# Gate and up weights of an expert loaded in four transfers of 1 MB instead of two of 2 MB

## What is computed

```python
    g_prob = jax.nn.softmax((t @ w_rg + b_rg).astype(jnp.float32), axis=-1)
    p_g, g_idx = lax.top_k(g_prob, 1)
    ...
    p_e, e_idx = lax.top_k(jax.nn.softmax(e_sel, axis=-1), TOP_K)
    ...
    for e in range(N_EXPERTS):
        hid = jax.nn.silu(t @ w_gate[e]) * (t @ w_up[e])
        y = y + ((hid * dense_w[:, e:e + 1]) @ w_down[e]).astype(jnp.float32)
```

## Time and profile before

| what | us |
|---|---|
| median of 3 runs | 1626.03 (1625.09 to 1627.09) |
| the profiled execution, its own time | 1628.22 |
| its span, first to last instruction | 1626.4 |
| first load issued by the loop over the ring | 1193.97 |
| last load of weights issued | 1583.16 |
| mean granted clock of TensorE, share of full | 0.962 |

### The profile page before, as it was taken

How to read it: one execution, slowest core, us unless ns; L and a number is a source line. 1 busy time by engine, 2 the same in 40 slices (tenths; PEclk the granted TensorE clock), 3 DMA queues, 4 the chain that set the end, 5 groups by cost and what they waited for, 6 DMA issues and landing times.

```text
span 1626.4 us, 28468 instructions
## 1 busy us (share of the span) xinstructions
PE 1491.8 (92%) x10825; PEld 1154.2 (71%) x10826; DVE 1005.2 (62%) x1858; ACT 702.5 (43%) x1216; POOL 67.3 (4%) x88
## 2 busy tenths in 40 slices
PE   8999999999999999999999999999989666676667
PEld 7888888888888888888888889887844333232333
DVE  6777788677777777788677777988643122212222
ACT  5555566555555555666455556846310000000000
POOL 0000040000001000030200000001000000000000
PEclk9999999999999999999999999999999788879888
DMA  9665374365555656373465545445999999999997
GB/s 318 208 205 181 113 239 136 106 224 187 193 181 179 209 181 196 94 245 116 154 218 194 180 173 169 160 139 188 389 391 427 429 429 428 429 428 429 428 429 310
DMA packets 153370, 407.86 MB, mean 251 GB/s; under 512 B 5712, under 2 KB 99264, under 8 KB 140000
## 3 DMA queue, kind: packets, MB, share of 16 engines
q1 hardware_dynamic: 151968, 404.28, 67.3%
q0 software_dynamic: 1344, 2.80, 0.8%
HBM read 406.00 MB, written 1.05 MB: 250 GB/s over the span
## 4 chain that ended last, share of the span: by engine, by line
PE 71%; DMA 20%; DVE 5%; ACT 2%; issue 1%; SPq 0%; DVEq 0%; ACTq 0%
PE bank L2107 20%; DMA expert_gu<-in_exp_gu 20%; PE bank L2113 10%; PE bank L2066 10%; PE bank L2067 10%; PE bank L2068 10%; PE bank L2726 4%; DVE wlo L1267 1%; PE bank L2738 1%; PE bank L2657 1%; PE bank L2681 1%; ACT hboth L820 0%; PE bank L2439 0%; DMA gcols<-in_gcols 0%; ACT whi L812 0%
## 5 line engine op out<-in xcount | busy, mean ns | idle before, releaser
L1267 DVE TENSOR_TENSOR wlo<-raw,whi 128x1024 fp32r<-128x1024 f32 (+1 forms) x396 | 449.1, 1182 | 65.0 <-ACT whi L812 64.8
L812 ACT ACTIVATE whi<-raw 128x1024 fp32r<-128x1024 f32 (+1 forms) x396 | 382.8, 1021 | 69.4 <-PE bank L2068 68.3
L2107 PE MATMUL bank<-hboth,whi 128*128 128x512 f32 x1408 | 350.5, 391 | 2.3 <-DVE hboth L1310 1.3
L2107 PEld LDWEIGHTS bank<-hboth,whi 128*128 128x128 f32 x1408 | 258.4, 188 | 53.8 <-ACT whi L812 2.0
L2726 PE MATMUL bank<-expert_gu,h_e 128*32 128x256 f32 x2048 | 166.8, 484 | 106.2 <-DMA expert_gu<-in_exp_gu 100.7
L2726 PEld LDWEIGHTS bank<-expert_gu,h_e 128*32 128x32 f32 x2048 | 75.0, 133 | 194.3 <-issue 113.5
L2113 PEld LDWEIGHTS bank<-hboth,wlo 128*128 128x128 f32 x1408 | 191.5, 190 | 13.4
L2113 PE MATMUL bank<-hboth,wlo 128*128 128x256 f32 x1408 | 195.7, 282 | 0.0
L2004 DVE SCALAR_TENSOR_TENSOR e_sg<-e_th,bank 128x128 f32<-128x128 f32 x33 | 9.5, 287 | 286.8 <-ACT e_th L1223 286.8
L2066 PE MATMUL bank<-whi,hboth 128*128 128x512 f32 (+2 forms) x384 | 150.2, 391 | 1.4 <-DVE hboth L1310 0.9
L2068 PE MATMUL bank<-whi,hboth 128*128 128x512 f32 (+2 forms) x384 | 146.9, 383 | 0.0
(11 more groups left out here) (388 smaller groups left out, 1772.6 us busy)
## 6 DMA issues: line engine op xcount, KB each, us to landing
expert_gu<-in_exp_gu SPq DMA_DIRECT2D x56, 2048.0 KB, 40.4
expert_dn<-in_exp_dn SPq DMA_DIRECT2D x31, 2048.0 KB, 41.0
raw<-in_ffn_w_gate SPq DMA_DIRECT2D x44, 1024.0 KB, 5.5
raw<-in_ffn_w_up SPq DMA_DIRECT2D x44, 1024.0 KB, 7.4
raw<-in_ffn_w_down SPq DMA_DIRECT2D x44, 1024.0 KB, 4.9
raw<-in_w_in SPq DMA_DIRECT2D x36, 1024.0 KB, 5.2
expert_gu<-in_exp_gu SPq DMA_DIRECT2D x11, 1024.0 KB, 9.7
raw<-in_w_o SPq DMA_DIRECT2D x8, 1024.0 KB, 5.5
```

The costliest lines, as they stand in the source:

```text
L812: nc.scalar.activation(slot_view(whi, slot, src), src, ACT.Copy).then_inc(hi_ready, inc)
L1267: nc.vector.tensor_tensor(slot_view(wlo, slot, src), src, slot_view(whi, slot, src).bitcast(F32), ALU.subtract).then_inc(lo_ready, inc)
L2107: nc.tensor.matmul(out_[:], wh[:, k, :], hboth[:, k, :, :], start=k == 0, stop=False, skip_group_check=True)
```

## The change

The two transfers of 2 MB become four of 1 MB, each of 2 of the 8 chunks. The semaphore `gu_half_done` becomes `gu_part_done`. It starts at 2 (an early matmul of the expert stage adds them) and every block adds 1 after each of chunks 1, 3 and 5, so that it stands at 3 x used + o once quarter o of the last block of the expert has been read, for o = 0, 1, 2; the fourth quarter waits for `gu_done` as before. The first two quarters signal `gu_landed[j]`, the last two `gu_rest_landed[j]`; PE still waits twice per block, for both quarters of a half together, which is why the values it waits for grow by 32 in a round instead of 16. Experts 0 to 2, the loads of down and the kept gate and up stay as they are, and so does the order of the loads.

```diff
-                n = KC * Q * P
-                sp.wait_ge(gu_half_done, used)
-                sp.dma_start(dst[:, 0:n], src[:, 0:n]).then_inc(gu_landed[j], 16)
-                sp.wait_ge(gu_done, used)
-                sp.dma_start(dst[:, n:2 * n], src[:, n:2 * n]).then_inc(gu_rest_landed[j], 16)
+                n = KC * Q * P // 2
+                for o in range(4):
+                    if o < 3:
+                        sp.wait_ge(gu_part_done, used * 3 + o)
+                    else:
+                        sp.wait_ge(gu_done, used)
+                    sp.dma_start(dst[:, o * n:(o + 1) * n], src[:, o * n:(o + 1) * n]).then_inc((gu_landed, gu_rest_landed)[o // 2][j], 16)
...
                         ins = nc.tensor.matmul(Y[2 * t + h][:], ident[:], x[:, t, h * 512:(h + 1) * 512], start=True, stop=False,
                                                skip_group_check=True)
+                        if (t, h) == (0, 0):
+                            ins.then_inc(gu_part_done, 2)
...
                     for c in range(KC):
+                        if c and c % 2 == 0:
+                            ins.then_inc(gu_part_done, 1)
                         if c == KC // 2:
-                            ins.then_inc(gu_half_done, 1)
...
-                        of = (ring_gu(g), (gu_landed[g], (round_ + 1) * 16), (gu_rest_landed[g], (round_ + 1) * 16))
+                        of = (ring_gu(g), (gu_landed[g], round_ * 32 + 16), (gu_rest_landed[g], round_ * 32 + 16))
```

More of the change, by code:

```diff
@@ L383, in program @@
         gu_rest_landed = [sem(f"gu_rest_landed{e}") for e in range(RING)]
-        gu_half_done = sem("gu_half_done")
+        gu_part_done = sem("gu_part_done")
         down_landed = [sem(f"down_landed{e}") for e in range(RING)]
```

## The result

| | before | after |
|---|---|---|
| median, us | 1626.29 (7 runs, 1624.54 to 1627.09) | 1630.46 (7 runs, 1629.68 to 1632.8) |
| ratio | | 1.0027, 95% interval 1.0018 to 1.0036 |
| span of the profiled execution, us | 1626.4 | 1628.8 |

The change makes the kernel 0.27% slower, some 4.2 us. The forecast was 1627.3 us and no difference; the measured time lies 0.4 us above the range's high end. In size it is rival (a): more is paid per piece in a full queue than I took. What the price is paid for is another matter, and experiment 2 decides it.

A forecast was written before the change was run, and what follows sets the result against it. The prediction took DMA transport at about 428 GB/s to bound the expert loop. From a median of 1626.03 us, 0.7 us gained at the entry and 2.0 lost to more transfers gave 1627.3 us, range 1624.7 to 1630.1.

The forecast's parts named there:

- rival (a): Full queue from 1206 us on: each further transfer costs 0.071 us at the DMA engines' change, 3.7 us slower; chance 0.20.
- What bounds the kernel: Expert loop: bound by transport at 4.895 us per 2 MB transfer, some eight queued; earlier issue wins only where the queue empties.
- Term 1, the entry: Loop entry: first load leaves 1.8 us earlier, down still waits for PE; gain 0.7 us, between 0 and 1.3.
- Term 2, the price of more transfers: Full stretch, experts 4 to 29: 52 more transfers at 0.039 us each lose 2.0 us, between 0 and 3.7.
- The six landings: 1 MB transfers landing from 1165.0 to 1179.9 us: 2.483 us each, giving the upper price of 0.071 us.
- Edits that cost nothing: SP's two more issues an expert, 0.34 us each, and the new waits: covered by 40.6 us of queue, no cost.
- (d): SP's issues: a queue taking only eight transfers delays the quarters, yet 26 us of cover keeps the forecast time; chance inside forecast's.
- The end: Last experts: down of expert 31 lands 2.4 us before it is needed, so its transfer stays hidden.
- (b): Loop entry: the holes in the rate close entirely, 3.3 us faster, 1622.7 us; chance 0.05.
- (c): Full stretch: a transfer's fixed part is not covered, 2.4 us for each of 52, 125 us lost, 1751 us; chance 0.01.

The follow-up runs named there:

- experiment 2: Kernel before, with the same 2 MB transfers but gate and up in HBM rows of 8 KB instead of 16 KB; 1630.12 us, ratio 1.0024.
- kernel 5: kernel 1 with SP also waiting, ahead of gate and up, for the landing of down two experts back; 1630.55 us, ratio 1.0029.
- kernel 6: Kernel before with SP also waiting, ahead of gate and up, for the landing of down two experts back; 1626.59 us, ratio 1.0004.
- kernel 1: Kernel before with each half of gate and up split into two 1 MB transfers, waits as before; 1630.18 us, ratio 1.0025.
- kernel 9: Changed kernel with quarters for expert 3 only, all later experts in two transfers of 2 MB; 1625.78 us, ratio 0.9998.
- 8, rows of 48 KB: Kernel before with experts 6 to 26 in one 6 MB transfer each, first and last rounds written out; 1624.43 us, ratio 0.9994; again 1624.38, 0.9990.
- 7, 32 and 16 KB: Kernel before with gate and up of experts 6 to 26 in one 4 MB transfer, first and last rounds written out; 1626.23 us, ratio 1.0003.
- kernel 4: Kernel before with gate and up in eight 512 KB transfers with 4 KB rows, waits as before; 1637.79 us, ratio 1.0069.

## Why the prediction was wrong, point by point

**What bounds the kernel**: right. The loop is bound by the transport; kernels 5 and 6 show that a shorter queue would do; in kernel 6 it is three to six transfers of 2 MB instead of eight.

**Term 1, the entry**: the mechanism was right. The first load leaves 1.7 us earlier (1.8 forecast), down stays where PE lets it, and the hole reopens before it. The size, 0.7 us of gain within 0 to 1.3, was not seen: the changed kernel and kernel 1, which lacks the earlier issue, are at 1.0027 and 1.0025, and kernel 9 is at 0.9998 with an interval wider than the term. The range's 1.3 us has no row either; the larger reading was 1.2 us.

**Term 2, the price of more transfers**: this is the step that failed, by its size. I took 0.039 us a transfer from a rate over 12 us, against 0.071 from the landings; measured are (14.835 - 14.685) / 2 = 0.075. So 52 transfers lose 3.9 us, not 2.0. The choice was made for the wrong reason, "the steadiest queue": a rate of three digits over 12 us carries an error as large as the difference of two such numbers, and the text said so two sentences earlier as the case for a bound of 0. The same stretch read from 1163.5 to 1175.5 us gives 424 GB/s and from 1165 to 1174 us 427, prices of 0.051 and 0.016 us. The six landings did little better: read to 0.1 us each, they give 0.071 with an error of up to 0.033. That the bound from them, 3.7 us, was nearly the answer, and with no gain at the entry gave the 1629.7 of rival (a), is in part luck.

**What is paid for** was left open between transfers and packets; the text went on to call it the price of a transfer, and rival (a) put it at each DMA engine's change from one transfer to the next. That place is wrong: kernel 2 makes no further change and pays the whole price. It is the packets:

| kernel | large packets per DMA engine and expert | transfers | us per expert |
|---|---|---|---|
| 8, rows of 48 KB | 8 | 1 | 14.535 |
| 7, 32 and 16 KB | 16 | 2 | 14.611 |
| before, 16 KB | 24 | 3 | 14.685 |
| 2, 8 KB in 2 MB transfers | 40 | 3 | 14.836 |
| after, 8 KB | 40 | 5 | 14.835 |
| 4, 4 KB | 72 | 9 | 15.134 |

From 8 packets to 72 it is 0.599 us for 64 packets, **9.4 ns each**, and every row lies within 0.002 us of that line. With no packets at all the line stands at 14.535 - 8 x 0.0094 = 14.460 us for 6.2915 MB, 435 GB/s.

**Edits that cost nothing**: the issues of SP did not stay at 0.34 us but grew to 1.9 in the median, since the queue takes in only so much. The landing forecast at near 40 us came at 31.5 for the same reason. (d) had foreseen a queue that holds SP back, though its cover was reckoned too high: eight transfers of that mix are at most 10.5 MB or 24.5 us, not 11 MB or 26 us. That it cost nothing all the same was argued in rival (d) and is shown by kernel 5.

**The end**: right. The chain behind the last landing is PE's, with no wait for down.

**Rivals**: (a) came true in its price, at 0.20, and not in its place. (b) and (c) are out, (b) by the changed kernel's own loss, (c) by the 424 GB/s. The 341 GB/s that the Trainium skill gives for transfers of 1 MB, weighed in the prediction, does not hold in this queue: the trace has 424. The Trainium skill ("DMA: Bandwidth & Descriptors", in the note on the measurements of section "Bandwidth") also has a price per packet: about 10.5 ns, seen there as a floor for tiny transfers of 64 packets. This case's traces agree in size, 9.4 ns, and show it with packets of 4 to 48 KB in a full stream; but the page doesn't say over how many engines its 64 packets are spread, and the small packets of this stream cost nothing to be seen, so the likeness may be chance. By the Trainium skill's 10.5 ns, taken per packet of an engine, 26 x 16 packets would have cost 4.4 us, as an estimate. The fabric ceiling of 435.2 GB/s that the Trainium skill gives on the same page, "Where 436 GB/s comes from", agrees with the line's 435.

**The range**: 1630.1 was too low by 0.4 us. It took the bound of the price without its own error, and the scatter of a median as 0.4 us where the interval of the ratio is 1.5 us to either side.

## What to carry to other kernels

In a stream of loads that fills the DMA, count the packets of each DMA engine, which are as long as the contiguous rows of a partition, and multiply by the price of one, here 9.4 ns; how many transfers they come in (three or five an expert), and how early they are issued, cost and won nothing here. Cutting a load finer can pay only where the queue runs dry (that it did was not seen here), and even there ask which later transfer is set by another engine, for the hole moves to just before it. Where two readings of one price differ by a factor of two, work out the error of each before choosing, and let the range follow the larger with its error.

## What the runs showed of the hardware that I had not expected

- A large packet takes 9.4 ns of its DMA engine's time on top of its bytes, whatever its length between 4 and 48 KB (whether in the engine or in HBM is open); the small packets at a transfer's end cost nothing to be seen (kernels 1 and 2 differ by two transfers an expert and 0.002 us).
- Packets follow the rows up to 48 KB; no limit was met.
- SP's issues are held up when the queue holds some hundred packets per DMA engine. Worked out from the time to landing: after, 31.5 us / 14.835 x 45 packets = 96, still taking issues one at a time; kernel 2 with its landing of 37.9 us and 43 packets, 110; kernel 4 with its median landing of 18.5 us and 81 packets, 99; before stood at 40.6 / 14.685 x 27 = 75 and was not held up. The exact limit stays open, and it costs no time.
- A stream of which two thirds come in transfers over 64 partitions, with the same rows, moves at 217 GB/s, 0.51 of full width, and slows the full-width transfers in it as well.
- Writing out two rounds of a loop cost 1.8 us (0.0002 to 0.0020 of the time), 0.8 of it outside the span.
